# A two-block transformer kernel: another way through the group norm of its recurrent stage, another order of the split product's matmuls, and norm roots read from PSUM

## The reference, cut to what matters

```python
def _rmsnorm(x, g):
    y = x * lax.rsqrt(jnp.mean(x * x, axis=-1, keepdims=True) + RMS_EPS)
    return y * g
...
    o = _wkv7_scan(rh, _heads(decay), kh, vh, kk, ah)
    mu = jnp.mean(o, axis=-1, keepdims=True)
    var = jnp.mean(jnp.square(o - mu), axis=-1, keepdims=True)
    o = ((o - mu) * lax.rsqrt(var + GN_EPS)).reshape(h.shape[0], h.shape[1], D_RWKV)
    o = o * ln_g + ln_b
    bonus = jnp.sum(rh * kh * r_k, axis=-1, keepdims=True) * vh
    o = o + bonus.reshape(o.shape)
    return o * g
```

## Time and profile before

| | us |
|---|---|
| median of 3 runs | 2042.65 |
| lowest and highest | 2041.98, 2044.66 |
| the profiled execution, its own time | 2044.09 |
| its span, first to last instruction | 2042.2 |
| TensorE busy in the span | 1973.1 (97%) |
| VectorE busy | 1025.6 (50%) |
| ScalarE busy | 787.8 (39%) |
| GpSimd busy | 898.6 (44%) |

### The profile page before, as it was taken

How to read it: one execution, slowest core, us unless ns; L and a number is a source line. 1 busy time by engine, 2 the same in 40 slices (tenths; PEclk the granted TensorE clock), 3 DMA queues, 4 the chain that set the end, 5 groups by cost and what they waited for, 6 DMA issues and landing times.

```text
span 2042.2 us, 40860 instructions
## 1 busy us (share of the span) xinstructions
PE 1973.1 (97%) x17144; PEld 1558.3 (76%) x17144; DVE 1025.6 (50%) x1747; ACT 787.8 (39%) x1298; POOL 898.6 (44%) x724
## 2 busy tenths in 40 slices
PE   6999999999999999998999999999999999999997
PEld 5876667887788888886777777777787888888886
DVE  6333453232741322577788888888425366322312
ACT  4456664223332322443444344434244244322321
POOL 5323365444454545445332333323243445545542
PEclk9989999999899999999999999999999999999999
DMA  8520012533332222241111111111132332223231
GB/s 337 186 73 22 12 52 96 187 110 102 125 122 95 98 98 93 94 142 55 41 57 49 42 46 51 49 49 34 60 138 81 126 104 90 96 94 103 93 103 63
DMA packets 53061, 187.20 MB, mean 92 GB/s; under 512 B 6032, under 2 KB 7184, under 8 KB 52624
## 3 DMA queue, kind: packets, MB, share of 16 engines
q1 hardware_dynamic: 49104, 174.49, 25.1%
q10 hardware_dynamic: 3776, 10.09, 1.4%
HBM read 178.27 MB, written 6.29 MB: 90 GB/s over the span
## 4 chain that ended last, share of the span: by engine, by line
PE 91%; DVE 4%; ACT 2%; issue 2%; POOL 1%; DMA 0%; DVEq 0%; SPq 0%; ACTq 0%
PE psum L913 25%; PE psum L915 23%; PE psum L914 23%; PE psum L1377 2%; PE psum L1059 2%; PE psum L1080 1%; PE psum L1065 1%; PE psum L1369 1%; PE psum L1353 1%; POOL wlo L789 1%; PE psum L1341 1%; PE psum L1309 1%; PE psum L1383 1%; PE psum L1098 1%; PE psum L1331 1%
## 5 line engine op out<-in xcount | busy, mean ns | idle before, releaser
L789 POOL TENSOR_TENSOR wlo<-raw,whi 128x512 fp32r<-128x512 f32 x524 | 713.7, 1383 | 925.9 <-ACT whi L1525 925.9
L913 PE MATMUL psum<-ah,whi 128*128 128x512 f32 x1256 | 523.4, 417 | 3.8 <-DVE ah L1965 3.0
L914 PE MATMUL psum<-ah,whi 128*128 128x512 f32 x1256 | 495.8, 395 | 0.0
L915 PE MATMUL psum<-ah,wlo 128*128 128x512 f32 x1256 | 495.3, 394 | 0.0
L1525 ACT ACTIVATE whi<-raw 128x1024 fp32r<-128x1024 f32 x262 | 275.9, 1054 | 324.0 <-PE psum L915 316.7
L913 PEld LDWEIGHTS psum<-ah,whi 128*128 128x128 f32 x1256 | 238.9, 190 | 66.7 <-issue 10.8
L915 PEld LDWEIGHTS psum<-ah,wlo 128*128 128x128 f32 x1256 | 239.2, 190 | 52.6
L914 PEld LDWEIGHTS psum<-ah,whi 128*128 128x128 f32 x1256 | 239.6, 191 | 43.8 <-issue 2.2
L913 PE MATMUL psum<-hidden,whi 128*128 128x512 f32 x536 | 208.7, 389 | 0.0
L915 PE MATMUL psum<-hidden,wlo 128*128 128x512 f32 x536 | 208.5, 389 | 0.0
L914 PE MATMUL psum<-hidden,whi 128*128 128x512 f32 x536 | 208.5, 389 | 0.0
(11 more groups left out here) (375 smaller groups left out, 2816.2 us busy)
## 6 DMA issues: line engine op xcount, KB each, us to landing
raw<-in_w SPq DMA_DIRECT2D x300, 512.0 KB, 3.5
raw_first<-in_w SPq DMA_DIRECT2D x14, 512.0 KB, 9.6
raw_ck<-in_w SPq DMA_DIRECT2D x8, 512.0 KB, 7.4
x<-in_x SPq DMA_DIRECT2D x4, 512.0 KB, 5.7
x_kept<-x ACTq DMA_DIRECT2D x1, 2048.0 KB, 10.0
ao_kept<-ao ACTq DMA_DIRECT2D x8, 256.0 KB, 2.3
aof<-ao_kept ACTq DMA_DIRECT2D x1, 2048.0 KB, 10.8
x<-x_kept ACTq DMA_DIRECT2D x1, 2048.0 KB, 8.4
```

What stands on the lines that cost most here:

```text
L789: pool.tensor_tensor(lo_weight(place(s))[:, c], raw_of(SPLITS[s])[:, c], hi_weight(place(s)).bitcast(F32)[:, c], ALU.subtract).then_inc(lo ...
L913: pe.matmul(dst, wh, h_, start=first, stop=False)
L914: pe.matmul(dst, wh, l_, start=False, stop=False)
L915: return pe.matmul(dst, wl, h_, start=False, stop=last)
```

## The change

Four things change.

- Group norm: "gnv" becomes one float32 product of the squares with `heads`, which leaves the sum over a head in every channel. ACT takes the root of it from PSUM into `sq[:, 1, :]` (128x512), with 1/64 as scale and the epsilon as bias. DVE takes the reciprocal of that in two halves of 128x256, two steps ("gnr", j, 0) and ("gnr", j, 1) at different places. "gnb" and `gnt` are gone. "gnend" multiplies with `sq[:, 1, :]` and moves from level 2 to level 3; the writing back of the result ("aoput") moves from level 3 to level 4.
- Taps: `TAPS` loses two in slot 2 and two in slot 8 and gains one in slot 4; ("conv", j, 1) ahead of level 1 becomes ("conv", j, 4).
- `three_as_made`: where a product follows the splitting of its activations, both matmuls with the high activation come first and wait only for the high part; the third, with the low activation, waits for the low part.
- Roots: for all norms over channels but "final" and "mix2", ACT reads the sums from PSUM and applies scale and epsilon in the root; `mean_square` is no longer called for them. Three constants for the epsilons are set by GpSimd at the start.

```diff
-TAPS = ((1, 0), (2, 0), (2, 0), (0, 0), (2, 0), (0, 0), (2, 0), (2, 0), (2, 0), (0, 1), (0, 0), (2, 0), (0, 1), (2, 0), (2, 0), (0, 3))
+TAPS = ((1, 0), (2, 0), (0, 0), (0, 0), (3, 0), (0, 0), (2, 0), (2, 0), (0, 0), (0, 1), (0, 0), (2, 0), (0, 1), (2, 0), (2, 0), (0, 3))
...
-        out += [("conv", j, 1)] if j else []
+        out += [("conv", j, 4)] if j else []
         for lv in range(1, LEVELS + 1):
             out += [("ip", j, 0, lv), ("ip", j, 1, lv)]
             if lv == 2 and j:
-                out += [("gnb", j - 1), ("gnend", j - 1)]
+                out.append(("gnr", j - 1, 1))
             out += slot()
             out += [("iy", j, 0, lv), ("iy", j, 1, lv)] + slot()
-            if lv == 3 and j:
+            if lv == 4 and j:
                 out.append(("aoput", j - 1))
             if lv < LEVELS:
-                out += [("inv", j, 0, lv), ("inv", j, 1, lv)] + slot()
+                out += [("inv", j, 0, lv), ("inv", j, 1, lv)]
+                if lv in (1, 3) and j:
+                    out.append(("gnr", j - 1, 0) if lv == 1 else ("gnend", j - 1))
+                out += slot()
...
-    behind = [[("gnm", KT - 1)], [("gnv", KT - 1)], [("gnb", KT - 1), ("gnend", KT - 1)], [("aoput", KT - 1)], [("aoload", KT - 1)], []]
+    behind = [[("gnm", KT - 1)], [("gnv", KT - 1)], [("gnr", KT - 1, 0), ("gnr", KT - 1, 1)], [("gnend", KT - 1)], [("aoput", KT - 1)], [("aoload", KT - 1)], []]
...
+            def three_as_made(dst, w, wcols, a, k, first, last, event):
+
+                wh, wl = hi_weight(w)[:, wcols], lo_weight(w)[:, wcols]
+                pe.wait_ge(hi_ready, EVENT[event] + 1)
+                pe.matmul(dst, wh, a[:, 0, k], start=first, stop=False)
+                pe.matmul(dst, wl, a[:, 0, k], start=False, stop=False)
+                pe.wait_ge(hl_ready, EVENT[event] + 1)
+                return pe.matmul(dst, wh, a[:, 1, k], start=False, stop=last)
...
-                elif kind == "gnb":
-                    pe.wait_ge(gnr_ready, j + 1)
-                    for t in range(TT):
-                        for hh in range(2):
-                            mm = pe.matmul(b[RN * hh:RN * hh + RN, t * P:t * P + P],
-                                           gnt[:, 2 * t + hh:2 * t + hh + 1].to_broadcast([P, RN]), eye, start=True, stop=True)
...
                     pe.wait_ge(gnsq_ready, j + 1)
-                    for t in range(TT):
-                        mm = pe.matmul(b[:, 2 * t:2 * t + 2], sq[:, 1, t * P:t * P + P], heads[:, ::RN], start=True, stop=True)
+                    mm = pe.matmul(b, heads, sq[:, 1, :], start=True, stop=True)
...
             def root(name):
-                wait_emptied(act, ("ss", name))
-                act.activation(roots(name), roots(name), ACT.Sqrt).then_inc(root_done, 1)
+                if name in ("final", "mix2"):
...
+                i = 1 if name == "conv" else 0
+                act.wait_ge(eps_ready, 3)
+                wait_filled(act, ("ss", name))
+                emptied_by(act.activation(roots(name), bank(("ss", name))[:, 0:TT], ACT.Sqrt, bias=eps[:, i:i + 1],
+                                          scale=1.0 / {"cq": QR, "ckv": KVR}.get(name, D)), ("ss", name))
...
                 elif kind == "gnv":
-                    wait_emptied(act, f)
-                    act.activation(gnt[:, :], gnt[:, :], ACT.Sqrt).then_inc(gnroot_done, 1)
+                    wait_filled(act, f)
+                    emptied_by(act.activation(sq[:, 1, :], bank(f), ACT.Sqrt, bias=eps[:, 2:3], scale=1.0 / RN), f)
...
             def normed(name, n, src, gain, dst, k0, tiles, bias=None, used=True):
-                mean_square(name, n)
                 inverse_root(name)
...
-                if k == 2:
-                    mean_square("mix", D)
                 if k == 4:
                     inverse_root("mix")
...
                 elif kind == "gnv":
-                    wait_filled(dve, f)
-                    if j:
-                        wait_filled(dve, ("gnb", j - 1))
-                    emptied_by(dve.tensor_scalar(gnt[:, :], bank(f)[:, 0:2 * TT], 1.0 / RN, GN_EPS, ALU.mult, ALU.add), f)
-                    dve.wait_ge(gnroot_done, j + 1)
-                    dve.reciprocal(gnt[:, :], gnt[:, :]).then_inc(gnr_ready, 1)
+                    pass
+                elif kind == "gnr":
+                    half = slice(S // 2 * f[2], S // 2 * f[2] + S // 2)
+                    wait_emptied(dve, ("gnv", j))
+                    dve.reciprocal(sq[:, 1, half], sq[:, 1, half]).then_inc(gnr_ready, 1)
                 elif kind == "gnend":
-                    wait_filled(dve, ("gnb", j))
-                    emptied_by(dve.scalar_tensor_tensor(og, og, vcol("ln_x_g_2", j), bank(("gnb", j)), ALU.mult, ALU.mult), ("gnb", j))
-                    wait_emptied(dve, ("gnb", j))
+                    dve.wait_ge(gnr_ready, 2 * j + 2)
+                    dve.scalar_tensor_tensor(og, og, vcol("ln_x_g_2", j), sq[:, 1, :], ALU.mult, ALU.mult).then_inc(gn_done, 1)
+                    dve.wait_ge(gn_done, j + 1)
```

More of the change, by code:

```diff
@@ L230 @@
 RKV_SLOT = {1: 0, 0: 1, 2: 0}
-IN_BANKS = ("lw2", "la2", "lg2", "kkss", "bonus", "tok", "inv", "akv", "ip", "iy", "tav", "st", "gnm", "gnv", "gnb")
+IN_BANKS = ("lw2", "la2", "lg2", "kkss", "bonus", "tok", "inv", "akv", "ip", "iy", "tav", "st", "gnm", "gnv")
 BLOCKS = weight_blocks()
@@ L515, in build_program @@
         modg = sb("modg", [P, 2 * KT])
-        sb("to_line", [P, 32 - TT])
+        eps = sb("to_line", [P, 32 - TT])[:, 0:3]
         psum = ctx.enter_context(nc.psum_tensor("psum", [P, 8, S], F32))
@@ L600, in build_program @@
             sw, cw, rate, kk = (work(n, S) for n in ("sw", "cw", "rate", "kk"))
-            gnt = work("gnt", 2 * TT)
             bv = work("bv", 2 * S)[:, :].rearrange("p (i s) -> p i s", i=2)
@@ L791, in weights_ahead @@
                     low[0] += 1
+            for i, value in enumerate((EPS, LN_EPS, GN_EPS)):
+                pool.memset(eps[:, i:i + 1], value).then_inc(eps_ready, 1)
             weights_ahead(1)
@@ L928, in product @@
                         pe.wait_ge(lo_done, 2 * s + 2)
-                    if event is not None:
-                        pe.wait_ge(hl_ready, EVENT[event + (i,)] + 1)
-                    mm = three(bank(name), place(s), slice(col0 + i * P, col0 + i * P + P), a, k, i == 0, i == len(kts) - 1)
+                    at = (bank(name), place(s), slice(col0 + i * P, col0 + i * P + P), a, k, i == 0, i == len(kts) - 1)
+                    mm = three(*at) if event is None else three_as_made(*at, event + (i,))
                 mm.then_inc(filled, 1)
@@ L947, in product_pair @@
                 for i in range(KT + lag):
-                    if i < KT:
-                        pe.wait_ge(hl_ready, EVENT[event + (i,)] + 1)
                     for name, k in zip(names, (i, i - lag)):
                         if 0 <= k < KT:
-                            mm = three(bank(name), place(SPLIT_AT[name]), slice(k * P, k * P + P), a, k, k == 0, k == KT - 1)
+                            mm = three_as_made(bank(name), place(SPLIT_AT[name]), slice(k * P, k * P + P), a, k, k == 0, k == KT - 1,
+                                               event + (k,))
                             if k == KT - 1:
@@ L1553, in root @@
             def root(name):
-                wait_emptied(act, ("ss", name))
-                act.activation(roots(name), roots(name), ACT.Sqrt).then_inc(root_done, 1)
+                if name in ("final", "mix2"):
+                    wait_emptied(act, ("ss", name))
+                    act.activation(roots(name), roots(name), ACT.Sqrt).then_inc(root_done, 1)
+                    return
+                i = 1 if name == "conv" else 0
[3 more added lines that the diff above has]
+                                          scale=1.0 / {"cq": QR, "ckv": KVR}.get(name, D)), ("ss", name))
             def high(event, dst, bias=0.0):
@@ L1871, in _ @@
                     wait_emptied(act, f)
+                    if j:
+                        act.wait_ge(gn_done, j)
                     act.activation(sq[:, 1, :], og, ACT.Square).then_inc(gnsq_ready, 1)
                 elif kind == "gnv":
-                    wait_emptied(act, f)
-                    act.activation(gnt[:, :], gnt[:, :], ACT.Sqrt).then_inc(gnroot_done, 1)
+                    wait_filled(act, f)
+                    emptied_by(act.activation(sq[:, 1, :], bank(f), ACT.Sqrt, bias=eps[:, 2:3], scale=1.0 / RN), f)
                 elif kind == "aoput":
@@ L1953, in inverse_root @@
             def inverse_root(name):
-                dve.wait_ge(root_done, [n for n, _ in NORMS].index(name) + 1)
+                if name == "final":
+                    dve.wait_ge(root_done, 1)
+                else:
+                    wait_emptied(dve, ("ss", name))
                 dve.reciprocal(roots(name), roots(name)).then_inc(rs_ready, 1)
@@ L2269, in roots_of_both @@
```

(3 more changed lines are left out.)

6 lines of the change are left out of this document (2 added, 4 removed).

## The result

| | before | changed |
|---|---|---|
| median of 14 runs, us | 2042.97 | 2047.99 |
| lowest and highest | 2041.30, 2044.73 | 2042.49, 2053.09 |
| profiled execution: its span | 2042.2 | 2050.9 |
| TensorE busy in the span | 1973.1 | 1974.1 |
| VectorE busy in the span | 1025.6 | 1038.3 |

The ratio is 1.0026 (95% interval 1.0016 to 1.0035), or +5.3 us (+3.3 to +7.2). The profiled execution, at 2052.74, is one of the longest of its runs. These runs of the changed kernel scatter over 10.6 us, those of the kernel before over 3.4.

What follows compares the result with a forecast made beforehand. TensorE was taken to bound the recurrent stage, busy 66.65 of 67 us per tile. Stage +3.1, clock +1.5 and norms -2.2 summed to +2.4 us on 2042.65: 2045.0 us, range for 8 in 10 2040.5 to 2051.0.

Steps and rivals of the forecast that it cites:

- group norm off TensorE: In each of 8 tiles, "gnb" gone and "gnv" shorter take 1.05 us from TensorE: 8.4 us in all.
- wait at level 1: TensorE's "iy" of level 1 waits 1.6 us for VectorE's "ip" in seven tiles: +11.2 us.
- wait at level 3: One tap more ahead of the "ip" of level 3 costs 0.05 us per tile: +0.35 us.
- falls of the clock: Half clock behind the level 1 waits, 1 in 5 each, likeliest one fall: +1.5 us, bounds 0 and +10.5.
- norms: Norms outside the recurrent stage: first MLP -1.05, second MLP -0.5, opening -0.45, last norm -0.2; together -2.2 us.
- The order of VectorE: At level 1, three more taps stand ahead of the "ip", done at 1152.2 when TensorE wants it at 1150.64.
- The pace of the taps: VectorE's taps follow at 0.79 us each; at 0.66 the wait would be 1.2 us, the total 2.7 lower.
- rival C: VectorE late at later levels too, meeting POOL's traffic: 0.5 to 1 us more per tile, 2047 to 2052; chance 0.10.
- A: The forecast case: level 1 wait of 1.6 us, zero to two clock falls, 2043.5 to 2046.5; chance 0.57.
- rival B: Clock falls behind three or more of the level 1 waits; three to five give 2048 to 2051; chance 0.18.
- D: Taps do not delay the "ip" of level 1, wait under 0.3 us: faster, 2032 to 2034; chance 0.10.
- E: Level 1 wait only 0.7 to 1.2 us, if `upad` or taps start earlier: -2 to -5; chance 0.05.

Runs made afterwards that it cites:

- second measurement: The changed kernel itself, unaltered, run again for a second profile; ratio 1.0021 (1.0011 to 1.0032) to the kernel before.
- group norm alone: The kernel before with only the new group norm and its taps, placed by VectorE's idle room, norms' edits undone: 2034.4 us, ratio 0.9954.
- filler in the wait: The changed kernel with three unread float32 products put ahead of TensorE's "iy" of level 1 in tiles 1 to 7: 2045.2 us, ratio 1.0005.
- three taps against four: The changed kernel with three taps ahead of level 1, one of its four moved ahead of the head sums: 2038.7 us, ratio 0.9980.
- edits alone: The kernel before with both norms' edits (product order, roots) and nothing else, measured twice: 2040.35 and 2040.10 us, ratio 0.9986 both times.
- first tap version: The changed kernel with three of the four taps ahead of level 1 moved behind it: 2033.8 us, ratio 0.9955 to the kernel before.
- taps by room: The changed kernel with three taps moved behind level 1, one of them to ahead of the head sums: 2031.1 us, ratio 0.9946.

## Why the prediction was right, and which terms were off

The forecast was +2.4 us, no change that a measurement can tell, by a gain and a loss of nearly one size. It measured +5.3 (+4.3 in the second measurement): inside the range for 8 in 10 as it was drawn, but above the +0.9 to +3.9 of the likeliest case. Term by term:

| term | predicted | measured | by |
|---|---|---|---|
| group norm off TensorE | -8.4 | -9.4, or -9.0 | group norm alone; its tiles: 7 x (65.17 - 66.30) - 1.05 = -9.0 |
| wait at level 1 | +11.2 | +12.2 | row of waits |
| wait at level 3 | +0.35 | 0 | no row |
| falls of the clock | +1.5 | +3.3 to +4.3 | filler in the wait; three taps against four: +3.9 |
| norms | -2.2 | -2.9, or -1.6 | edits alone; with and without the rest |
| sum | +2.4 | +3.2 to +5.9 | |

The last tile's 1.05 us was not measured by itself; it stands in the table as it was worked out.

**The order of VectorE** was the step that decided, and it held. By the working the first "ip" starts 0.72 + 0.85 + 2.37 = 3.94 us behind `upad`; the rows say 1154.69 - 1150.74 = 3.95. The wait came out 1.75 and not 1.6, for two small reasons: `upad` starts 0.45 us ahead of TensorE's "ip" (1151.19 - 1150.74) and not 0.53, and the half that TensorE waits for ends at about 1155.1, 0.15 us before TensorE starts, where the working allowed almost nothing.

**The pace of the taps**: the three take 1154.69 - 1152.32 = 2.37 us, 0.79 each, and the wait is 1.75 and not 1.2. With three taps ahead instead of four the wait was 0.95, shorter by 0.80, the pace of one tap. In the first tap version two instructions of "gnend" that wait for one another follow after 0.79 us too (1169.58, 1170.37), and the instruction behind one that nobody waits for (L2318, 1162.25) after 0.67. What the Trainium skill says in "VectorE: DVE Perf Modes", section "The DRAIN you can't avoid", that a semaphore after each operation costs nothing extra, is not what these rows show.

**The gain** came as worked out: "gnb" gone, "gnv" shorter by 0.04. A further 0.07 us per tile (the group norm alone) to 0.16 (most tiles of the taps by room) appears later in the tile and is unexplained.

**Later levels.** There was no further wait in the changed kernel, so rival C fell, though by luck of the order: TensorE's own wait at level 1 gives VectorE the room behind it. With the wait taken away the late places do show (0.63 us in one tile of the first tap version), and there it was GpSimd's traffic that rival C named.

**The clock** is the term that was mis-sized. "1 in 5 per wait, likeliest one fall" rested on one fall behind 1.33 us and none behind 1.67, both in tile 0 among smaller matmuls. Two profiles showed 4 and 2 falls of 7, and the filler puts the mean at two to three, +3.3 to +4.3 us. So what came lay between A and the lower edge of rival B (three falls, 2048); the mechanism was right, and so was the price of one fall, 1.5 us. The evidence from tile 0 was also that of one execution: there TensorE waits 3.11 us ahead of the place at 938 us, which left the clock at 1.00 before and did not in the two profiles of the changed kernel. Before, then changed:

```profile
934.36 1.10 PE L1309 MATMUL psum<-lh,lwt 128*128 128x512 f32 x2 [3.11 <-ACT lh L1812]
```

```profile
935.93 2.05 PE L1320 MATMUL psum<-lh,lwt 128*128 128x512 f32 x2 [3.11 <-ACT lh L1823]
...
938.00:940.00 2.00, 2.00 (x5) 0.86 (x5) 1.19 (x3) 1.86 (x4) 1.83 (x2) 0.50 0.54 188
```

That fall cost nothing: from this row to the `kh` matmuls (L1341, L1346) both take 8.01 us, since the slower matmuls fill waits of 1.67 and 1.21 us that TensorE had there at the full clock. Behind level 1 there was nothing to fill. The Trainium skill's "TensorE: Matmul & The Clock Gate", section "HAM oscillation — how this bites in real kernels", tells of a kernel in which the wait for data lets the clock fall at every turn of a loop. Here it was not every turn, and not the same turns twice.

**The norms** were near in sum, with parts off by more. High part first gives 0.9 at the first MLP (predicted 0.85), and at the second 0.46: from the product's first matmul to the one behind it 1701.53 - 1695.24 = 6.29 us before and 1710.30 - 1704.47 = 5.83 after (predicted 0.5). The roots give 0.08 and not 0.2 at the first MLP and at the last norm, whose spread starts 1.74 us behind its sums instead of 1.82. VectorE's scaling of 128x4 was a short instruction, and ScalarE's wait for PSUM takes its place. In the opening the gain was there and went again. TensorE's spread and its second column sums, before and changed:

```profile
15.37 2.08 PE L995 MATMUL psum<-eye_ones,rs 128*128 128x128 f32 x8 [1.25 <-DVE rs L1955]
...
22.89 1.01 PE L1113 MATMUL psum<-eye_ones,mod_sums 128*128 128x1 f32 x4 [4.43 <-DVE mod_sums L2024]
...
32.13 0.39 PE L913 MATMUL psum<-ah,w_ahead 128*128 128x512 f32 x1
```

```profile
14.91 2.08 PE L1006 MATMUL psum<-eye_ones,rs 128*128 128x128 f32 x8 [0.62 <-DVE rs L1971]
...
22.32 1.01 PE L1124 MATMUL psum<-eye_ones,mod_sums 128*128 128x1 f32 x4 [4.42 <-DVE mod_sums L2039]
...
32.14 0.63 PE L918 MATMUL psum<-ah,w_ahead 128*128 128x512 f32 x1
```

At 22 us the changed kernel is 0.57 us ahead, although its column sums began 0.17 later: the roots give 0.74 here, more than the 0.45 of the prediction, and the same in every profile that has them. At 32 us its matmuls still take 0.63 us, those of before already 0.39: the clock rose 2 us later in this execution. The clock's first rise lies anywhere between 26 and 35 us in the profiles here. By the first MLP's sums, at about 512 us, the profiles lie between 498.1 and 501.1 us behind their opening sums, with the old roots (499.1 to 500.7) as with the new, so what is left of the 0.74 can't be read from them.

**Rivals.** D, faster because the taps do not delay the "ip", did not come; the runs show that it was one table of numbers away, at 0.9946. Its "about 0.4 us", below which the kernel would be over 0.2% faster, was a slip: by the prediction's own terms 7 x (wait - 1.05) - 1.05 - 2.2 reaches -4.1 at 0.93 us, and three taps ahead, with a wait of 0.95, did measure 0.9980. E fell with the wait's size.

## What to carry to other kernels

Where a fixed order feeds two engines, count from the last thing that the first engine must have to the first thing that the second one wants: what stands between them costs its full length, less the room that was there, while a few instructions later the same work can be free. Place movable work by the idle time in front of each hand-over, and leave some of it, since operations of the late engine now and then take longer. A wait on TensorE is not priced by its length alone: behind the waits of 1.7 us here the clock fell in some executions and not in others. One profile therefore says little of the mean; that takes medians of two kernels that differ in the idleness alone, as with the filler.

## What the runs showed of the hardware

- Seven waits of 0.94 to 0.96 us, each behind full matmuls, left the granted clock at 1.00 in the one profile of them. Of waits of 1.70 to 1.75 us four of seven were followed by 0.50 in one profile and two of seven in another; of waits of 1.88 to 1.98 us four of seven. A wait of 3.11 us in tile 0, the same in all kernels here, was followed by 1.00 in nine profiles and by 0.50 in four.
- The same VectorE instruction on the same operands had several durations: the scan 1.23, 1.33, 1.53 or 2.28 us, the multiplication by the gate 0.69 or 1.65. They go with GpSimd's `wlo`: an instruction that starts within one ends 1.07 to 1.08 us (the scan) or 0.55 us (the multiplication) behind GpSimd's end. The kernel before paid for this in each of tiles 1 to 7 (scan 2.33 us), the changed kernel less (1.54), since its scan meets the `wlo` later; neither the prediction nor the change aimed at it.
- Two edits that measured 0.9999 and 1.0001 alone measured 0.9986 together, twice. The rows at their places explain about 1.5 us of it, 2.3 with the opening's 0.74; with intervals of almost 2 us either way the three figures do not contradict one another, and whether the rest is more than scatter stays open.
